# Two attentions in one kernel: one distance table for all heads, and another order of the maxima, inverses and last transfers

## The chip, the cores and the metric

The kernel runs on one core of a Trainium2 chip, as one launch. The core has five engines with queues of their own: PE (TensorE), DVE (VectorE), ACT (ScalarE), POOL (GpSimd) and SP (SyncE, which here only issues transfers). The metric is the device time of one execution in microseconds; of several runs the median is taken.

## The reference

Two transformer blocks work on 1024 tokens of width 1024, in float32. The first block (forgetting attention, a convolution, pooling, a feed-forward part) is not touched. The second has two attentions side by side, whose results go through a gate each, are added and projected:

```
# differential attention, 4 heads, two maps (c) a head, all 1024 keys
s = einsum(q, k) * scale - slope[h] * |qpos - kpos|      # slope[h] = 4 ** -(h + 1)
p = softmax(s);  a = p[0] - lam * p[1];  y_a = rmsnorm(a @ v)
# neighbourhood attention, 8 heads, a grid of 16 x 64 tokens,
# each query sees 8 rows x 16 columns of keys
s = einsum(q, k) * scale + bias[h];  p = softmax(s);  y_b = p @ v
merged = g_a * (y_a @ w_branch_a) + g_b * (y_b @ w_branch_b)
```

## The kernel before, in words

Every engine's program is written out by hand as a sequence of methods, one for each stage (`pe_att2`, `act_att2`, ... and then `pe_na`, `act_na`, ...); semaphores are the only coupling between the engines. An instruction that waits holds everything behind it in its engine's queue. Weights are split into a high and a low part, so that a product of float32 accuracy is three matmuls: `w_load` on SP fetches a tile, `w_high` on ACT rounds it, `w_low` on DVE or POOL takes the rest (`low_engines` says which).

**Differential attention** (`*_att2`). There are 32 units, 8 blocks of 128 queries for each of 4 heads. For each unit PE forms the scores of both maps (16 matmuls), DVE adds the distance table `tab` and takes the row maximum in one instruction (`maxes`, calling `negmax`), ACT takes the exponentials, DVE joins the maps, PE transposes, ACT and DVE copy, PE multiplies with the values. The gate products (`gate_steps`, 24 matmuls a unit, one PSUM bank) lie between these as filling. `tab` holds slope times distance, so each head has another one: SP loads it in `sp_att2` when the last maximum of the head before has read the old one. The queries were scaled in `dve_proj2`.

**Neighbourhood attention** (`*_na`). There are 64 `unit`s (8 blocks of queries for each of 8 heads) that only yield the row maxima: PE forms scores, DVE adds the table `tabS` and takes the maximum. For every four units (a group g) DVE splits the four maxima (`halves`), PE transposes them (`rows` on PE), and DVE writes them (`rows` on DVE) as further rows of the tile `stk`, from which the second pass subtracts them inside the product. The second pass has 96 `step`s, six a group, 12 a head: PE forms transposed scores in one of three banks, DVE adds the table `tabT` (`add`), ACT takes the exponential, and PE multiplies with the values three steps later (`value`), into bank 4 or 5 by group; ACT copies a finished bank (`taken`). Units of group g + 2 are done among the steps of group g, at steps 2 to 5 of the six. From unit 4 on they share banks 6 and 7 with the transposed maxima, and so a unit waits until DVE has read these.

The softmax is divided late: POOL stores a head's row sums to HBM and reads them back spread over the partitions (`sums`), DVE takes the reciprocal (`inverse`), POOL stores it and reads it back broadcast (`inverses`), DVE multiplies (`share`), and every second head ACT and DVE split the result (`high`, `mixed`). All are put at fixed steps.

Between the steps go `branch` parts, by `branch_places`: the norm of the first attention's result and then the 64 parts of its product (`wa`, 16 halves `a` of 4 parts). DVE multiplies each half in bank 3 by its gate half in `gab`, POOL stores it (`scr_yaw`), and only then SP loads the gate half for half a + 2 (`g_load`, `scr_g`). The last 11 parts lie behind the 96 steps, in `branch(192)`. Behind that stands `pe_wb`, the second attention's product and the sum of both; its first parts don't need the last head, its later ones do.

## Time and profile before

| | us |
|---|---|
| median of 3 runs | 3134.53 (3132.15 to 3135.2) |
| the profiled execution | 3132.92 |
| its span | 3131.1 |
| granted clock, mean over the span | 0.965 of full |
| differential attention | about 1586 to 1919 |
| neighbourhood attention | about 1914 to 2175 |
| product of the second branch | about 2175 to 2224 |

A time in the trace counts from the start of the span, on the profiled execution. "Busy" is the time in which an engine's instructions run; for PE it is too high where a matmul stands alone, since the ends are modelled. A wait such as `A <- B` says that A stood until B was done.

### The profile page before, as it was taken

How to read it: one execution, taken by the hardware profiler on the slowest of the kernel's cores; microseconds unless marked ns; L12 is line 12 of the kernel's file. 1: busy time of each engine (PE TensorE's matmuls, PEld its weight loads, DVE VectorE, ACT ScalarE, POOL GpSimd, SP SyncE). 2: the span in 40 equal slices, each digit the busy share in tenths (PEclk: the TensorE clock that was granted, in tenths of full speed). 3: DMA queues.
4: the chain of work that ended last, by engine and by line, in shares of the span. 5: the costliest groups of instructions: out<-in, count | busy, mean ns of one | idle time of the engine just before them, and what ended most of it. 6: DMA issues, size and time to landing. Idle time of an engine off the chain costs nothing.

```text
span 3131.1 us, 31288 instructions
## 1 busy us (share of the span) xinstructions
PE 2934.1 (94%) x13012; PEld 2365.2 (76%) x13012; DVE 1437.4 (46%) x1672; ACT 945.5 (30%) x1193; POOL 360.9 (12%) x309
## 2 busy tenths in 40 slices
PE   7988999999999999899999998887978999999996
PEld 5777767788888888688877786655766888888874
DVE  5775454453535454533244445664554313333335
ACT  3212442221212122311355565432342221111123
POOL 2223111000000000200012221112320000000003
PEclk9999999999999999899999999998998999999997
DMA  2123432111111111246313334553521111111113
GB/s 103 62 74 117 133 92 95 49 46 55 42 53 41 57 38 51 98 141 214 115 64 107 105 104 144 171 163 126 193 88 54 39 56 43 59 34 61 48 60 122
DMA packets 89085, 275.04 MB, mean 88 GB/s; under 512 B 12648, under 2 KB 15336, under 8 KB 88944
## 3 DMA queue, kind: packets, MB, share of 16 engines
q1 hardware_dynamic: 74448, 226.66, 22.2%
q0 software_dynamic: 14496, 46.38, 4.2%
q8 instruction: 103, 1.69, 0.2%
q14 instruction: 38, 0.31, 0.0%
HBM read 220.40 MB, written 52.59 MB: 87 GB/s over the span
## 4 chain that ended last, share of the span: by engine, by line
PE 76%; DVE 8%; ACT 4%; issue 4%; DMA 3%; POOL 1%; SPq 0%; DVEq 0%; ACTq 0%; POOLq 0%
PE ps L206 75%; DVE cacc L177 2%; DVE YA L174 1%; ACT PB L171 1%; PE ps L209 1%; DMA tab<-in_alibi 1%; ACT AH L171 1%; DMA small<-scr_sum 1%; ACT wh L171 1%; DMA scr_sum<-YS 1%; DVE PB L177 1%; DVE stk L174 0%; DVE wl L174 0%; POOL wl L174 0%; DVE XR L174 0%
## 5 line engine op out<-in xcount | busy, mean ns | idle before, releaser
L206 PE MATMUL ps<-AH,wh 128*128 128x512 f32 (+1 forms) x2240 | 900.9, 402 | 80.2 <-DVE wl L174 31.6
L206 PE MATMUL ps<-AL,wh 128*128 128x512 f32 (+1 forms) x2240 | 883.3, 394 | 0.0
L206 PE MATMUL ps<-AH,wl 128*128 128x512 f32 (+1 forms) x2240 | 882.0, 394 | 0.0
L174 DVE TENSOR_TENSOR wl<-raw,wh 128x1024 fp32r<-128x1024 f32 (+2 forms) x240 | 280.5, 1169 | 835.8 <-ACT wh L171 835.6
L206 PEld LDWEIGHTS ps<-AH,wh 128*128 128x128 f32 (+1 forms) x2240 | 425.4, 190 | 190.5 <-issue 41.5
L171 ACT ACTIVATE wh<-raw 128x1024 fp32r<-128x1024 f32 (+2 forms) x289 | 261.8, 906 | 793.6 <-PE ps L206 783.3
L206 PEld LDWEIGHTS ps<-AH,wl 128*128 128x128 f32 (+1 forms) x2240 | 425.6, 190 | 93.3
L206 PEld LDWEIGHTS ps<-AL,wh 128*128 128x128 f32 (+1 forms) x2240 | 426.5, 190 | 90.6 <-issue 3.7
L206 PE MATMUL ps<-UH,wh 128*128 128x512 f32 x880 | 346.8, 394 | 12.6 <-DVE wl L174 7.6
L206 PE MATMUL ps<-UL,wh 128*128 128x512 f32 x880 | 345.1, 392 | 0.0
L206 PE MATMUL ps<-UH,wl 128*128 128x512 f32 x880 | 344.7, 392 | 0.0
L206 PE MATMUL ps<-stk,stk 128*128 128x512 f32 (+3 forms) x832 | 257.6, 422 | 38.8 <-DVE small L186 21.0
L206 PEld LDWEIGHTS ps<-stk,stk 128*128 128x128 f32 x832 | 151.5, 197 | 111.9 <-issue 36.8
L206 PEld LDWEIGHTS ps<-UH,wh 128*128 128x128 f32 x880 | 167.0, 190 | 51.7 <-issue 11.1
L174 POOL TENSOR_TENSOR sqacc<-sqacc,sq 128x512 f32<-128x512 f32 (+1 forms) x51 | 88.1, 1728 | 934.7 <-ACT sq L171 929.9
L206 PEld LDWEIGHTS ps<-UH,wl 128*128 128x128 f32 x880 | 166.9, 190 | 35.1
L206 PEld LDWEIGHTS ps<-UL,wh 128*128 128x128 f32 x880 | 167.0, 190 | 34.4
L174 POOL TENSOR_TENSOR wl<-raw,wh 128x1024 fp32r<-128x1024 f32 (+3 forms) x49 | 109.0, 2226 | 318.2 <-ACT wh L171 318.1
L177 DVE SCALAR_TENSOR_TENSOR cv<-ub,vec,cv 128x1024 f32<-128x1024 f32 x88 | 113.1, 1285 | 55.2 <-ACT cv L171 53.7
L197 DVE RECIPROCAL small<-small 128x1 f32<-128x1 f32 (+3 forms) x61 | 11.4, 186 | 207.8 <-ACT PB L171 129.8
L177 DVE SCALAR_TENSOR_TENSOR cacc<-hp,vec,cacc 128x1024 f32<-128x1024 f32 x60 | 102.0, 1700 | 1.8
L213 POOL DMA_DIRECT2D scr_x<-XR x8 | 4.5, 565 | 715.1 <-DVE XR L174 715.1
(198 smaller groups left out, 3113.4 us busy)
## 6 DMA issues: line engine op xcount, KB each, us to landing
raw<-in_w_up SPq DMA_DIRECT2D x44, 512.0 KB, 3.3
raw<-in_w_gu SPq DMA_DIRECT2D x44, 512.0 KB, 3.2
raw<-in_w_w2in SPq DMA_DIRECT2D x32, 512.0 KB, 4.2
raw<-in_w_down SPq DMA_DIRECT2D x56, 256.0 KB, 2.6
raw<-in_w_down SPq DMA_DIRECT2D x32, 320.0 KB, 2.8
xin<-in_xT SPq DMA_DIRECT2D x16, 512.0 KB, 4.4
stk<-scr_ka SPq DMA_DIRECT2D x32, 256.0 KB, 8.0
raw<-in_w_w2v SPq DMA_DIRECT2D x16, 512.0 KB, 3.3
```

Of the source, the lines that this page charges most:

```text
L171: return Issued(self, self.e.activation(out, in_, func, **kw))
L174: return Issued(self, self.e.tensor_tensor(out, a, b, op))
L177: return Issued(self, self.e.scalar_tensor_tensor(out=out, in0=a, scalar=s, in1=b, op0=op0, op1=op1))
L197: return Issued(self, self.e.reciprocal(out, a))
L206: return Issued(self, self.e.matmul(out, l, r, start=start, stop=stop))
L209: return Issued(self, self.e.transpose(out, a, ident))
L213: return Issued(self, self.e.dma_start(out, in_))
```

## The change

One table of distances (4^-1 times distance) serves all four heads: the queries of head h are scaled by a further 4^h, and the maximum is taken with a scale of -4^-h, so that the sum comes out as before. The gate's fifth step (k = 4) of the last unit moves from the next stage to behind its transposes. In the neighbourhood attention `na_behind` gives the places of units, halves, transposes and rows; the transposed maxima go to banks 4 and 5. Inverses, shares and second splits come some steps later. Behind the steps POOL does the last head's sums and inverse ahead of its branch parts, DVE has an order written out by hand, half 14 of the branch product gets bank 2, and one low part moves from POOL to DVE. The loads of the next stage wait for the last broadcast.

```diff
@@ -116,7 +116,7 @@
     for s in range(len(TILES)):
-        on = "p" if 1 <= s <= TILE["wout", 0] or g0 < s <= wb0 else "d"
+        on = "p" if 1 <= s <= TILE["wout", 0] or g0 < s < wb0 else "d"
         count[on] += 1
@@ -181,9 +181,9 @@
-    def negmax(self, out, a, b, low):
-        return Issued(self, self.e.tensor_tensor_reduce(out=out, in0=a, in1=b, scale=-1.0, scalar=3.0e38, op0=ALU.add,
+    def negmax(self, out, a, b, low, scale=1.0):
+        return Issued(self, self.e.tensor_tensor_reduce(out=out, in0=a, in1=b, scale=-scale, scalar=3.0e38, op0=ALU.add,
                                                         op1=ALU.min, accum_out=low))
@@ -1597,7 +1597,8 @@
             q.wait_ge(S.bl, n - 1)
-            q.stt(self.T2[b][:, :], self.pair(b), 0.125 if key[0][0] == "q" else 1.0, self.RB[:, :], ALU.mult,
+            scale = {"qa": 0.125 * 4.0 ** key[1], "qb": 0.125}
+            q.stt(self.T2[b][:, :], self.pair(b), scale[key[0]] if key[0] in scale else 1.0, self.RB[:, :], ALU.mult,
                   ALU.mult).then_inc(S.bev)
@@ -1637,9 +1638,10 @@
                 self.stack_load(q, self.stk2[2], 2, "qa", "ka", S.dstk2)
-                q.dma(self.tab[:, :], self.io["alibi"][0, :, :]).then_inc(S.dtab0, 16)
+                q.dma(self.tab[:, :], self.io["alibi"]).then_inc(S.dtab0, 16)
         for key in self.SWEEPS2:
@@ -1700,8 +1702,7 @@
             turn(u)
-            if u < 31:
-                self.gate_steps(q, u, 4, 8)
+            self.gate_steps(q, u, 4, 8 if u < 31 else 5)
         value(15)
@@ -1762,13 +1763,14 @@
                 q.wait_ge(S.sc, 64 + 2 * u + c + 1)
-                q.wait_ge(S.dtab0, 16 * (h + 1))
+                q.wait_ge(S.dtab0, 16)
                 q.wait_ge(S.dqs0, 256)
...
                 q.wait_ge(S.cc, u - 1)
-                q.negmax(self.PB2[j][:, :], self.pair(c), self.tab[:, at:at + NTOK], m[:, 0:1]).then_inc(S.mx)
+                q.negmax(self.PB2[j][:, :], self.pair(c), self.tab[:, at:at + NTOK], m[:, 0:1],
+                         4.0 ** -h).then_inc(S.mx)
@@ -1842,9 +1844,6 @@
                 self.w_load(q, TILE["w2in", ("g", u // 2)] + 3)
-            if i == 7 and h < 3:
-                q.wait_ge(S.mx, 64 + 2 * (u + 1) + 2)
-                q.dma(self.tab[:, :], self.io["alibi"][h + 1, :, :]).then_inc(S.dtab0, 16)
         self.na_tab(q, 0)
@@ -1927,7 +1926,7 @@
         S = self.S
-        q.wait_ge((S.dtab0, S.dtab1)[h % 2], (64 if h % 2 == 0 else 0) + 32 * (h // 2) + 16 * part)
+        q.wait_ge((S.dtab0, S.dtab1)[h % 2], (16 if h % 2 == 0 else 0) + 32 * (h // 2) + 16 * part)
@@ -1952,9 +1951,23 @@
+    @staticmethod
+    def na_behind(n):
+        g, r = n // 6, n % 6
+        unit = n + 4 if n < 12 else 4 * g + 8 + r if r < 4 and g < 14 else None
+        halved = {4: 1, 8: 2, 12: 3}[n] if n in (4, 8, 12) else g + 2 if r == 4 and 2 <= g < 14 else None
+        turned = {4: 1, 9: 2, 12: 3}[n] if n in (4, 9, 12) else g + 2 if r == 5 and 2 <= g < 14 else None
+        rows = {5: 1, 10: 2, 13: 3}[n] if n in (5, 10, 13) else g + 1 if r == 1 and 3 <= g < 15 else None
+        return unit, halved, turned, rows
...
-        return self.bank((4, 5)[g] if g < 2 else 6)
+        return self.bank((4, 5, 4, 4)[g] if g < 4 else 4 + (g + 1) % 2)
+    def wa_out(self, a):
+        return self.bank(2 if a == 14 else 3)
@@ -1969,7 +1982,6 @@
                 q.wait_ge(S.ya, 16)
-                q.wait_ge(S.qmr, 8 + u // 4 if u >= 12 else 0)
             out = self.na_out(u)
@@ -1982,6 +1994,8 @@
             self.turned_wait(q, self.CN2 + 63)
+            q.wait_ge(S.qmr, 8 + g)
+            q.wait_ge(S.tyc, 8 + (g - 2 if g >= 4 else 1 if g > 1 else 0))
             q.transpose(self.na_turned(g)[:, 0:128], f32(self.mcN[:, :]), self.ident).then_inc(S.mtr)
@@ -2004,7 +2018,7 @@
             q.wait_ge(S.vone, 2)
-            q.wait_ge(S.qmr, 8 + 2)
+            q.wait_ge(S.qmr, 8 + (g + 1 if g < 2 else min(g + 2, 16)))
             q.wait_ge(S.tyc, 8 + g - 1)
@@ -2033,35 +2047,35 @@
                     q.wait_ge(S.bspl, k + 1)
-                    q.wait_ge(S.wsm, a)
-                    ws = slice(k * P, k * P + P)
-                    q.mm(self.bank(3), h[:, ws], self.Ah[k][:, HALF[half]], k == 0, False)
-                    q.mm(self.bank(3), h[:, ws], self.Al[k][:, HALF[half]], False, False)
-                    i = q.mm(self.bank(3), l[:, ws], self.Ah[k][:, HALF[half]], False, k == 3)
+                    q.wait_ge(S.wsm, a - (a == 14))
+                    if a == 14:
+                        q.wait_ge(S.tad, 96)
+                    ws, out = slice(k * P, k * P + P), self.wa_out(a)
+                    q.mm(out, h[:, ws], self.Ah[k][:, HALF[half]], k == 0, False)
+                    q.mm(out, h[:, ws], self.Al[k][:, HALF[half]], False, False)
+                    i = q.mm(out, l[:, ws], self.Ah[k][:, HALF[half]], False, k == 3)
                     if k == 3:
...
             unit(u)
-            self.gate_steps(q, 31, 4 + u, 5 + u)
-        unit(4)
+            if u < 3:
+                self.gate_steps(q, 31, 5 + u, 6 + u)
         rows(0)
-        for u in (5, 6, 7):
-            unit(u)
         for n in range(99):
-            g = n // 6
+            u, _, g, _ = self.na_behind(n)
             if n < 96:
                 step(n)
-                if n % 6 > 1 and g < 14:
-                    unit(4 * g + 6 + n % 6)
+                if u is not None:
+                    unit(u)
                 branch(2 * n)
...
                 branch(2 * n + 1)
-            if n % 6 == 0 and g < 15:
-                rows(g + 1)
+                if g is not None:
+                    rows(g)
         branch(192)
@@ -2113,8 +2127,8 @@
                 branch(2 * n + 1)
-            if n >= 37 and n % 24 == 13:
-                high((n - 37) // 24)
+            if n >= 43 and n % 24 == 19:
+                high((n - 43) // 24)
         branch(192)
@@ -2181,6 +2195,12 @@
+        def product(a):
+            n, half = a // 2, a % 2
+            q.wait_ge(S.gem, GEM[TILE["wa", n], half])
+            q.wait_ge((S.dsp0, S.dsp1)[half], 48 + 16 * (n + 1))
+            q.tt(self.gab[half], self.wa_out(a), self.gab[half], ALU.mult).then_inc(S.wsm)
@@ -2203,41 +2223,37 @@
                 if part == "wa" and b == 3:
-                    n, half = a // 2, a % 2
-                    q.wait_ge(S.gem, GEM[TILE["wa", n], half])
-                    q.wait_ge((S.dsp0, S.dsp1)[half], 48 + 16 * (n + 1))
-                    q.tt(self.gab[half], self.bank(3), self.gab[half], ALU.mult).then_inc(S.wsm)
+                    product(a)
...
         halves(0)
-        unit(4)
         rows(0)
-        for u in (5, 6, 7):
-            unit(u)
-        halves(1)
         for n in range(96):
-            g = n // 6
+            u, halved, _, g = self.na_behind(n)
             add(n)
-            if n % 6 > 1 and g < 14:
-                unit(4 * g + 6 + n % 6)
-            if n % 6 == 0 and 1 <= g < 15:
-                halves(g + 1)
+            if u is not None:
+                unit(u)
+            if halved is not None:
+                halves(halved)
+            if g is not None:
+                rows(g)
             branch(2 * n)
-            if n % 6 == 1 and g < 15:
-                rows(g + 1)
-            if n >= 18 and n % 12 == 6:
-                inverse((n - 18) // 12)
-            if n >= 24 and n % 12 == 0:
-                share((n - 24) // 12)
-            if n >= 38 and n % 24 == 14:
-                mixed((n - 38) // 24)
+            if n >= 22 and n % 12 == 10:
+                inverse((n - 22) // 12)
+            if n >= 30 and n % 12 == 6:
+                share((n - 30) // 12)
+            if n >= 44 and n % 24 == 20:
+                mixed((n - 44) // 24)
             branch(2 * n + 1)
+        product(13)
+        self.w_low(q, TILE["wb", 0])
         share(6)
-        branch(192)
         inverse(7)
+        product(14)
+        product(15)
         share(7)
@@ -2267,7 +2283,7 @@
                     n, half, k = a // 2, a % 2, b
-                    if half == 0 and k == 2:
+                    if half == 0 and k == 2 and n < 7:
                         self.w_low(q, TILE["wa", n] + 1)
@@ -2277,12 +2293,12 @@
                 sums((n - 15) // 12)
-            if n >= 19 and n % 12 == 7:
-                inverses((n - 19) // 12)
+            if n >= 23 and n % 12 == 11:
+                inverses((n - 23) // 12)
             branch(2 * n + 1)
-        branch(192)
         sums(7)
         inverses(7)
+        branch(192)
@@ -2420,6 +2436,7 @@
             q.wait_ge(S.wsm, 16)
+            q.wait_ge(S.dinv, 32 * 16)
             q.wait_ge(S.dyw0, 16 * (n + 1))
@@ -2579,7 +2596,7 @@
         S = self.S
-        return (S.dstk0, S.dstk1, S.dtab0, S.dtab1)[n % 4], (864, 864, 192, 128)[n % 4]
+        return (S.dstk0, S.dstk1, S.dtab0, S.dtab1)[n % 4], (864, 864, 144, 128)[n % 4]
@@ -3039,11 +3056,8 @@
-    al = np.zeros((4, P, 1920), np.float32)
     dist = np.abs(np.arange(P)[:, None] + 896 - np.arange(1920)[None, :]).astype(np.float32)
-    for h in range(4):
-        al[h] = -(2.0 ** (-8.0 * (h + 1) / 4)) * dist
-    a["alibi"] = al
+    a["alibi"] = -(2.0 ** (-8.0 / 4)) * dist
```

## Rows read from the trace of the kernel before

**Rows 1.** The page, engines: busy us, share of the span, instructions.

```profile
PE 2934.1 (94%) x13012; PEld 2365.2 (76%) x13012; DVE 1437.4 (46%) x1672; ACT 945.5 (30%) x1193; POOL 360.9 (12%) x309
```

**Rows 2.** The chain of waits in the differential attention: start us, us, what.

```profile
1642.28 10.75 PE ps L206 x48
...
1689.41 10.74 PE ps L206 x48
...
1729.81 10.74 PE ps L206 x48
...
1775.90 10.75 PE ps L206 x48
...
1816.30 10.75 PE ps L206 x48
...
1858.41 10.75 PE ps L206 x48
```

**Rows 3.** Waits in the differential attention: us, times, longest.

```profile
DVE PB L186 <- DMA tab<-in_alibi: 16.4, 3, 6.4
```

**Rows 4.** Windows: length, busy PE, PEld, DVE, ACT, POOL, clock, DMA share, GB/s.

```profile
1972.35:1989.47 17.12, 15.33 (x72) 12.07 (x71) 11.48 (x26) 8.93 (x14) 1.08 (x2) 0.80 0.06 17
2028.18:2043.10 14.92, 10.82 (x44) 7.26 (x43) 7.85 (x19) 3.74 (x7) 2.76 (x5) 1.00 0.45 172
2043.10:2054.84 11.74, 11.33 (x47) 7.78 (x46) 8.92 (x19) 4.12 (x8) 2.34 (x3) 1.00 0.96 272
2054.84:2072.04 17.20, 13.60 (x44) 9.26 (x43) 8.23 (x19) 4.26 (x8) 3.42 (x5) 0.80 0.29 108
2084.74:2099.54 14.80, 12.38 (x44) 8.30 (x43) 8.07 (x20) 4.26 (x8) 2.88 (x4) 0.88 0.44 167
2111.98:2123.11 11.13, 10.58 (x44) 7.22 (x43) 8.12 (x21) 4.26 (x8) 3.54 (x6) 1.00 0.31 96
```

**Rows 5.** Waits in the neighbourhood attention: us, times, longest.

```profile
DVE small L197 <- DMA small<-scr_sum: 24.6, 6, 12.1
...
PE ps L206 <- DVE stk L174: 14.5, 10, 3.4
```

**Rows 6.** Timeline of the tail: start, us, what, [idle before <- releaser].

```profile
2142.43 0.60 ACT L171 ACTIVATE YS<-ps 128x512 f32<-128x512 f32 x1 [2.27 <-PE ps L206]
...
2145.51 0.54 POOL L213 DMA_DIRECT2D scr_yaw<-yb  x1 [4.65 <-DVE yb L174]
...
2153.72 0.51 POOL L213 DMA_DIRECT2D scr_sum<-YS  x1
2159.86 0.58 POOL L213 DMA_DIRECT2D small<-scr_sum  x1 [5.63 <-DMA scr_sum<-YS]
...
2167.43 0.53 POOL L213 DMA_DIRECT2D RBc<-scr_inv  x1 [1.41 <-DMA scr_inv<-small]
...
2164.98 0.20 DVE L197 RECIPROCAL small<-small 128x8 f32<-128x8 f32 x1 [12.10 <-DMA small<-scr_sum]
2170.74 1.22 DVE L174 TENSOR_TENSOR RBc<-YS,RBc 64x1024 f32<-64x1024 f32 x1 [5.56 <-DMA RBc<-scr_inv]
...
2175.06 0.77 PE L206 MATMUL ps<-AH,wh 128*128 128x512 f32 x1 [18.82 <-DVE wl L174]
```

**Rows 7.** Timeline of the prologue, SyncE and VectorE.

```profile
1928.85 0.37 SPq L213 DMA_DIRECT2D tabT<-in_nak  x1
...
1935.48 0.69 DVE L174 TENSOR_TENSOR XT<-ps,tabT 128x512 f32<-128x512 f32 x1
```

**Rows 8.** The tile tabT, before 1934 us.

```profile
DMA to landing us min/median/max: 4.3/4.3/4.3
```

**Rows 9.** The tile tabS, whole span: ns min/median/max.

```profile
L186 DVE CUSTOM_DVE_ANT_0 ps<-ps,tabS x64: 685/761/833, 1923.8 to 2121.1; 128x512 f32<-128x512 f32 x32, 128x640 f32<-128x640 f32 x32
...
DMA to landing us min/median/max: 5.2/9.0/13.7
```

**Rows 10.** Timeline of SyncE in the loop.

```profile
2083.46 0.38 SPq L213 DMA_DIRECT2D tabS<-in_na  x1
```

## The prediction

> **What bounds the kernel now.** The page first: PE is busy 94% of the span [rows 1], so time is to be had only where PE stands still, or runs at its lower clock, and the change touches one stretch of that kind, from the differential attention at 1586 us to the restart of the branch products at 2175 us. Three views show three kinds of loss in it.
>
> In the differential attention the chain of waits has a beat: the group of 48 matmuls begins every 20.20 us, two units of work (1689.41 to 1729.81 is 40.40, two beats) [rows 2]. Three beats are longer, and the waits say why: VectorE stood 16.4 us in 3 stalls for the distance table [rows 3].
>
> In the neighbourhood loop no engine is full. Groups of six steps take 11.1 to 17.2 us [rows 4]. The undisturbed ones, such as 2043.10 to 2054.84, take 11.7 with VectorE 8.9 and PE 11.3 busy (PE's busy time is inflated where matmuls stand alone, its weight loads are busy 7.8). The long ones have VectorE standing in the reciprocal for a transfer (24.6 us in 6 waits, the longest, 12.1, in the tail: 12.5 in the loop) and PE standing for the rows that VectorE writes into `stk` (14.5 us in 10 waits) [rows 5], and two of them have a granted clock of 0.80, a part of them at 1.2 GHz after PE stood still [rows 4].
>
> In the tail PE stands 18.8 us in one piece, to 2175.06 [rows 6]. Behind that is a chain: POOL issues head 7's row sums at 2153.72 although ScalarE had copied them by 2143.03, because the stores of the branch products stand ahead of them in POOL's queue; readback at 2159.86, reciprocal at 2164.98, broadcast issued at 2167.43, share at 2170.74, then the two splits and the weight's low half [rows 6].
>
> **Part 1, one table.** Three of four table loads go, and the maximum is scaled by 4^-h instead, in the same instruction, and the queries by 4^h, also in an instruction that is there: 0 us added, 64 maxima and 16 scalings unchanged in number and shape. Removed: from 1642.28 to 1689.41, from 1729.81 to 1775.90 and from 1816.30 to 1858.41 the chain needed 47.13, 46.09 and 42.11 for two beats that elsewhere take 40.40 [rows 2]: 6.73 + 5.69 + 1.71 = 14.1 us. That is less than the 16.4 that VectorE stood, since PE had gate matmuls to do under the start of each stall, and it includes what the clock lost afterwards. What is late next is the ordinary beat itself. The stack loads for the head after next stay where they are, with a whole head (four beats, 81 us) to land in. I take -14, bounds -14.5 and -11 (if a stack or weight load were hidden under the stall).
>
> **Part 2, the seam.** One of four gate steps (3 matmuls at 0.23 us, 0.7 us) moves from behind the last value product to ahead of it, where PE waits about a microsecond for the copies: -0.7. The neighbourhood prologue keeps units 0 to 3 and the first rows; units 4 to 7 go into steps 0 to 3. The first addition ran at 1935.48; its key table was issued at 1928.85 [rows 7] and landed in 4.3, at 1933.2 [rows 8]. That issue stands behind the last store of the differential attention, which a slightly earlier gate moves forward by about 1 us, so the first addition can come at about 1932, 3.5 us sooner. But 12 units instead of 8 now lie in the first two groups, and a unit's maximum is 0.76 us of VectorE [rows 9] and the read of its result 0.14: 3.6 us given back where VectorE has no room, nothing where it has (it waited for PE between the small steps). Of 4.2 gained I keep 2. Bounds -5 and +2, the latter if `rows` for group 1, which now has its transpose in step 4 and its product in step 5 right ahead of step 6, stalls each engine once more.
>
> **Part 3, the loop.** Reciprocals come 4 steps later (n = 22 + 12h instead of 18), shares 6, the second split 6. The sums are issued at step 15 + 12h; from there to the reciprocal were 3 steps, some 6 us, for a round trip of about 10 (in the tail 2153.72 to 2164.96 [rows 6]); now it is 7 steps, some 14 us. So the stalls go whole. The shares then have 7 steps for the inverse's store and broadcast (from the reciprocal at 2164.98 to the share at 2170.74, 5.8 us [rows 6]), and the copies of the next head but one stand two steps behind the share that frees their buffer: no new wait. POOL's `inverses` moves with them, and what queues behind it there is a branch store or a weight's low half, each with a tile's time (about 19 us) to spare. Compare groups: the odd ones take 14.92, 17.20, 14.80 and 11.13, the last with 0.6 of stall, thus 10.5 undisturbed; together 58.05 - 42.0 = 16 over that level. The group at 1972.35 took 17.1 with 11.5 of VectorE work at clock 0.80 [rows 4]; at 14.0 it gives 3. Together 19. The new places of the maxima (units in steps 0 to 3, where value products are small, instead of 2 to 5; the turned maxima in a value bank, so that no unit waits for `rows`) take a PE wait of a few tenths to a microsecond from each of 12 groups: 0.5 each, 6 us. What they add is waits on the copy of a value bank three steps earlier, met by then. I take -25. Bounds: -12, if only the 12.5 of reciprocal stalls goes and all else stays; -38, if eleven groups came down to the 10.3 of the densest work.
>
> A rule speaks here against me. In the loop the granted clock was 1.00 in undisturbed groups in spite of PE pauses up to 1 us at every step, and below it only in groups with a long stall [rows 4]. The Trainium skill, "TensorE: Matmul & The Clock Gate", section "A second HAM failure mode: psum-queue depth-cycling", says that frequent small idle times between groups of matmuls, with the banks cycled, make the clock swing between its two levels by themselves; the steps here cycle three banks. By the trace the clock's loss goes with the stalls; by the rule it stays, and that is the first rival.
>
> **Part 4, the tail.** Now POOL does sums and inverse of head 7 first, and the branch stores last. Sums at 2143.1 instead of 2153.7; with the old durations (to the readback 6.1, to the reciprocal 5.1, to the broadcast 2.5, landing 3.3) readback 2149, reciprocal 2153.5 to 2154, broadcast 2156, landed 2159.5. VectorE meanwhile does product 13, then stands in `inverse(7)` with products 14 and 15 behind it. PE has product 14 ready in its own bank by 2147.2, and then waits for the evacuation: about 7 us idle; product 15 (12 matmuls, 2.7 us, up to 5.5 at 1.2 GHz) ends at 2157 to 2160. A second wait is new: the gate half for product 15 is loaded only when the store of product 13 has landed, and that store is now behind the broadcast in POOL's queue: issued 2156.5, landed 2158.8, load landed about 2162 (before, the store went at 2145.51 [rows 6]). So product 15 ends at about 2162.7, share at 2164, both splits and the low half as before 4.3 us later: PE restarts at about 2167 instead of 2175. The 18 matmuls that are possible before fit in 2160 to 2165, so what follows restarts at the full clock more likely than now, worth up to 2. The low half that moves to VectorE is 0.7 us in its waiting time. The first loads of the mixing stage wait for the last broadcast and product 15 and go at 2163 instead of 2153, used from 2171: 8 us for what landed within 4 to 9. I take -10; bounds -13 (the gate half is no wait) and 0 (these loads are late).
>
> **Sum.** 14 + 3 + 25 + 10 = 52 against the profiled execution's own 3132.9, thus 3081. The median of the runs is 1.6 higher, 3134.5, so I forecast 3082.5 for a median. Everything behind 2190 us is untouched.
>
> **Rivals,** each with the time of a median.
> First, the loop gives little: the clock goes on falling by itself (the rule above), or the reciprocal wait is replaced by one on a bank or table. For it: VectorE waits for PE in nearly every step. Against: the undisturbed groups are already the pattern that is left. Loop -12, the rest as above: 39 less, 3095.
> Second, the tail only shifts: the new order puts VectorE's wait ahead of two products and the gate half behind a store, so that PE's idle time is split and the clock is low for more of it. For it: the wait for the store above. Tail 0: 42 less, 3092.
> Third, slower: the loads of a head's table become the bound of the loop. `tabS` is issued by SP behind the gate halves, in the trace as late as 2083.46 for step 62 [rows 10], and landing takes 5.2 to 13.7 us [rows 9]; the first unit of the head needs it two steps earlier than before, and the steps are faster. At the old pace it had 17 us; now about 13. A stall begins where issue is 4 us later or landing exceeds 13, and it comes out slower than before only if each of six heads stands 9 us or more. Price at 10 us a head: 60 against 52 gained, 3143. Against: the transfers' share in an undisturbed group is only 0.31 to 0.96 [rows 4], and a single late landing costs 1 to 3.
> Fourth, the table's stall was not the table's (a queue behind it holds all): 14 come back, 3096. Against: [rows 3] name the transfer, all three times at a head's start.
>
> **Chances.** Forecast (3070 to 3091) 0.60; first rival 0.15; second 0.08; third 0.03; fourth 0.03; more than forecast, down to 3060, 0.06; both of the first two 0.05 (3105). Range 3063 to 3106. What a measurement of this kernel tells from no change is about 0.2%, 6 us. Faster 0.95, same 0.02, slower 0.03.
>
> **What would show it.** No wait on `tab`, and a beat of 20.20 through all heads. Reciprocals in the loop without a transfer as releaser; groups of 10 to 12.5 us; clock near 1.00 from 1950 on. In the tail sums right behind the copy, PE idle twice (about 7, then a few us) instead of 18.8 once. Wrong would be: an XT or `ps` wait on `tabS` or `tabT`, groups still over 14 us, or PE restarting later than 10 us behind the broadcast's landing.

## The result, and the profile after

The changed kernel takes 3095.65 us (median of 4 runs, 3094.52 to 3098.76), the kernel before, on the same chip, 3134.86. The ratio is 0.9878, with a 95% interval of 0.9861 to 0.9895: 39.2 us less, where 52 had been forecast. The profiled execution took 3094.52 (span 3092.7, mean granted clock 0.969), and the lines of this section are its trace against the one of before. One execution of e11, an experiment further down, ran in a slow state (4194.22 us at a mean granted clock of 0.65) and is left out of its median; all others compared here are fast.

The page's engines, which answer to [rows 1]:

```profile
PE 2924.6 (95%) x13012; PEld 2357.9 (76%) x13012; DVE 1434.8 (46%) x1673; ACT 944.8 (31%) x1193; POOL 360.3 (12%) x308
```

The work is the same; what has changed is where it stands still. Four checkpoints divide the gain. The first maximum of the differential attention comes at 1584.05 (before 1586.09; nothing ahead of it was changed, so its 2.0 us are scatter). From there to the first addition of group 2 of the neighbourhood loop it is 358.10 us (before 372.69), from there to the loop's last addition 170.94 (before 180.75), from there to the product of the second branch 30.29 (before 42.31). That is 14.6 + 9.8 + 12.0 = 36.4 us, and with the scatter the 38.4 by which the spans differ. Behind that checkpoint both take the same (949.3).

The chain of waits in the differential attention, which answers to [rows 2], now has the one beat of 20.20 us throughout, and the wait of [rows 3] is gone:

```profile
1640.26 10.74 PE ps L206 x48
1660.46 10.75 PE ps L206 x48
1680.66 10.74 PE ps L206 x48
1700.86 10.75 PE ps L206 x48
1721.06 10.74 PE ps L206 x48
```

The seam, SyncE and VectorE (start, us, what, and in brackets the idle time and what ended it), to compare with [rows 7]. The first addition is 3.3 us earlier, counted from the first maximum and without the table's part, and now waits for its table, which lands 4.4 us behind its issue (4.3 before, [rows 8]):

```profile
1911.63 0.37 SPq L213 DMA_DIRECT2D tabT<-in_nak  x1
...
1912.87 0.69 DVE L174 TENSOR_TENSOR stk<-ps,cst 64x512 fp32r<-64x512 f32 x1 [0.42 <-PE ps L209]
1916.06 0.69 DVE L174 TENSOR_TENSOR XT<-ps,tabT 128x512 f32<-128x512 f32 x1 [2.50 <-DMA tabT<-in_nak]
```

Windows of five groups of the loop (columns as in [rows 4]), groups 3 and 8 to 11. The long ones of 14.92, 17.20 and 14.80 that a transfer had stopped (groups 7, 9 and 11 of before) are 11.95, 11.67 and 14.27 now; but no group with maxima in it is shorter than 11.6 us, group 3 is still 17.2 at a clock of 0.80, and the ones that had been undisturbed have not gained (group 8, 11.74 before, is 12.03):

```profile
1956.08:1973.26 17.18, 15.44 (x72) 11.89 (x71) 11.12 (x26) 9.16 (x14) 0.99 (x2) 0.80 0.01 0
...
2022.29:2034.32 12.03, 11.07 (x47) 7.86 (x46) 7.71 (x18) 4.15 (x8) 2.88 (x4) 1.00 0.88 217
2034.32:2045.99 11.67, 10.94 (x44) 7.14 (x43) 8.75 (x20) 4.15 (x8) 1.66 (x3) 1.00 0.55 210
2045.99:2058.61 12.62, 11.06 (x47) 7.86 (x46) 7.75 (x18) 3.63 (x7) 2.91 (x4) 1.00 0.71 194
2058.61:2072.88 14.27, 12.54 (x44) 8.17 (x43) 10.13 (x22) 5.17 (x9) 2.86 (x4) 0.88 0.46 166
```

The waits of the neighbourhood attention in the kernel after (us, times, longest), to compare with [rows 5]: of 24.6 us for the row sums 1.2 are left (in the tail), and PE's 14.5 us for `stk` don't appear. In their place stands a wait for L186, the maximum of a unit (PEld, the weight loads, and PE, the matmuls, overlap, so the two rows are not added up):

```profile
PEld ps L206 <- DVE small L186: 28.0, 28, 2.9
...
PE ps L206 <- DVE small L186: 16.5, 23, 2.4
...
DVE small L197 <- DMA small<-scr_sum: 1.2, 1, 1.2
```

The same view of before has less than half of it:

```profile
PEld ps L206 <- DVE small L186: 11.8, 13, 1.6
...
PE ps L206 <- DVE small L186: 6.7, 11, 1.3
```

The tail after, to compare with [rows 6]. POOL issues the sums at 2118.18; readback, reciprocal, inverse and broadcast follow within 8 us. VectorE then stands 8.4 us before the last product, until its gate half has landed, and PE, which had stood 18.82 us once, stands 3.53 and 3.52:

```profile
2118.18 0.50 POOL L213 DMA_DIRECT2D scr_sum<-YS  x1
...
2121.44 0.59 POOL L213 DMA_DIRECT2D small<-scr_sum  x1 [2.77 <-DMA scr_sum<-YS]
2123.40 0.20 DVE L197 RECIPROCAL small<-small 128x8 f32<-128x8 f32 x1 [1.17 <-DMA small<-scr_sum]
...
2124.22 0.80 PE L206 MATMUL ps<-AH,wh 128*128 128x512 f32 x1 [3.53 <-DVE yb L174]
...
2125.87 0.54 POOL L213 DMA_DIRECT2D RBc<-scr_inv  x1 [1.42 <-DMA scr_inv<-small]
2126.40 1.11 POOL L213 DMA_DIRECT2D scr_yaw<-yb  x2
...
2132.59 0.69 DVE L174 TENSOR_TENSOR yb<-ps,yb 128x512 f32<-128x512 f32 x1 [8.41 <-DMA yb<-scr_g]
...
2137.63 0.77 PE L206 MATMUL ps<-AH,wh 128*128 128x512 f32 x1 [3.52 <-DVE wl L174]
```

### The profile page after: what moved, and what is told of

It reads as the page before. It is cut to its first block, busy times and chain, and to the rows that moved or that the text cites. A ratio compares the mean times of both kernels' runs of the same rounds, so it can differ in the third digit from the quotient of the medians.

```text
span 3092.7 us, 31280 instructions
## 1 busy us (share of the span) xinstructions
PE 2924.6 (95%) x13012; PEld 2357.9 (76%) x13012; DVE 1434.8 (46%) x1673; ACT 944.8 (31%) x1193; POOL 360.3 (12%) x308
## 4 chain that ended last, share of the span: by engine, by line
PE 78%; DVE 9%; ACT 4%; issue 3%; DMA 1%; POOL 1%; SPq 0%; DVEq 0%; POOLq 0%; ACTq 0%
PE ps L206 77%; DVE cacc L177 1%; DVE YA L174 1%; ACT PB L171 1%; PE ps L209 1%; ACT AH L171 1%; DVE PB L177 1%; DVE ps L186 1%; DVE stk L174 1%; DVE XT L174 1%; DVE wl L174 0%; ACT wh L171 0%; DVE XR L174 0%; DMA raw<-in_w_w2out 0%; DVE AL L177 0%
## 5 line engine op out<-in xcount | busy, mean ns | idle before, releaser
L206 PE MATMUL ps<-stk,stk 128*128 128x512 f32 (+3 forms) x832 | 250.9, 413 | 24.7 <-DVE small L186 21.7
L197 DVE RECIPROCAL small<-small 128x1 f32<-128x1 f32 (+3 forms) x61 | 11.3, 186 | 193.3 <-ACT PB L171 139.5
```

Source lines behind the costliest of these rows:

```text
L197: return Issued(self, self.e.reciprocal(out, a))
L206: return Issued(self, self.e.matmul(out, l, r, start=start, stop=stop))
```

## The experiments

Twelve runs (e1 to e12) were made in three sessions, each beside the kernel before on the same chip; the changed kernel's own result has a session of its own, in which the kernel before took 3134.86. Ratios are to the kernel before of the session; "loop" is the time from the first to the last addition of the 96 steps in the profiled execution, "tail" from there to VectorE's first product of the second branch. Loop and tail are read from one trace a kernel. Four traces with the changed kernel's loop (changed, e4, e5, e8) have 197.0 to 197.6, so there the loop is read closely. Two with the loop of before (before, e1) have 204.05 and 209.2: where transfers stop it, it is not. Medians are compared within a session, ratios across; where e3 and e4 are set against the changed kernel both are given.

| kernel | median us | ratio (95%) | loop | tail |
|---|---|---|---|---|
| before | 3134.3, 3136.5, 3133.6 | 1 | 204.05 | 42.3 |
| changed | 3095.65 | 0.9878 (0.9861 to 0.9895) | 197.03 | 30.3 |
| e1 one table alone | 3119.55 | 0.9953 (0.9936 to 0.9970) | 209.2 | 41.2 |
| e2 old order of maxima | 3091.72 | 0.9864 (0.9844 to 0.9885) | 191.2 | 30.2 |
| e3 early inverses | 3096.77 | 0.9886 (0.9868 to 0.9904) | 206.9 | 29.0 |
| e4 old tail | 3108.27 | 0.9925 (0.9904 to 0.9946) | 197.5 | 46.3 |
| e5 changed again | 3095.53 | 0.9867 (0.9850 to 0.9883) | 197.06 | 32.2 |
| e6 maxima spread | 3077.94 | 0.9814 (0.9797 to 0.9831) | 179.9 | 30.0 |
| e7 maxima late | 3086.27 | 0.9846 (0.9827 to 0.9865) | 189.6 | 30.2 |
| e8 another tail | 3092.88 | 0.9863 (0.9848 to 0.9878) | 197.6 | 25.7 |
| e9 spread and tail | 3077.58 | 0.9825 (0.9800 to 0.9849) | 179.1 | 29.5 |
| e10 narrow units in one bank | 3089.21 | 0.9862 (0.9841 to 0.9884) | 193.8 | 31.9 |
| e11 all three | 3073.89 | 0.9810 (0.9787 to 0.9834) | 178.4 | 27.5 |
| e12 splits late, units not | 3093.94 | 0.9878 (0.9855 to 0.9901) | 196.0 | 32.3 |

### The parts, one by one (first session)

**e1** is the kernel before with one table (the edits to `alibi`, `negmax`, the queries' scale and the counts of its semaphore, nothing else).

> The kernel before with the one distance table alone. My theory, from the chain of waits in both traces (14.1 us between the same two places): 3134.9 - 14 = 3120.7, 3119 to 3122.5. Rival (the table's stall hid other loads that now come late, or the saving is partly the clock's and comes back elsewhere): 3124 or more.

Measured: 14.7 us less than before, inside the 3119 to 3122.5 that had been expected. Its waits have none for `tab`. The theory of the table holds, and the fourth rival falls.

**e2** is the changed kernel with the places of units, halves and rows of before (prologue too) and the turned maxima in bank 6; late inverses and the new tail stay.

```diff
-        return self.bank((4, 5, 4, 4)[g] if g < 4 else 4 + (g + 1) % 2)
+        return self.bank((4, 5)[g] if g < 2 else 6)
...
-                if u is not None:
-                    unit(u)
+                if n % 6 > 1 and g < 14:
+                    unit(4 * g + 6 + n % 6)
```

> The changed kernel with the old places of the maxima, halves and rows (units in steps 2 to 5, turned maxima in bank 6, units 4 to 7 and the gate's fifth step in the prologue). Theory A: the new order gained nothing in the loop, because four units in four steps running through one pair of banks make PE wait for each maximum, and VectorE then stands at the end of the group: 3095.6, within 3 either way; groups of six steps 11.5 to 12.5 us, waits PE <- small shorter and PE <- stk longer than in the changed kernel. Rival B (my prediction's term): the new order is worth 6 us and more, 3101 to 3104.

Measured: no loss at all; by the ratios it is 4.4 us below the changed kernel, with intervals that overlap, so rival B falls. Its loop is 5.8 us shorter than the changed kernel's (4.6 of them from group 2 on), though it has PE's waits for `stk` (4.6 us), which the new order takes away; its wait for the maxima is 6.4 us against 16.5. The first addition comes 4.7 us later (336.7 against 332.0 behind the first maximum), since four more units stand ahead of it. So the new order of the loop takes away a wait and brings a larger one, and from the first maximum to the last addition the two orders differ by 1.2 us only.

**e3** puts inverses, shares and second splits back to their early steps.

```diff
-            if n >= 22 and n % 12 == 10:
-                inverse((n - 22) // 12)
+            if n >= 18 and n % 12 == 6:
+                inverse((n - 18) // 12)
```

> The changed kernel with reciprocals at step 18 + 12h, shares at 24, splits at 37 and 38 as before. Theory A (the late inverses are the whole of the loop's gain of about 10, the stalls of 12.5 us come back): 3106 to 3110, VectorE again waiting for small<-scr_sum 10 to 13 us in the loop and one or two more stretches at 1.2 GHz. Rival B (the order carries part of the gain, the stalls hide behind PE): 3098 to 3102.

Measured: 3096.77, below what both theories gave (3106 to 3110, 3098 to 3102), and by the ratios 2.5 us above the changed kernel, within the intervals. In its profiled execution (the slowest of its five, 3102.08) the loop is 9.9 us longer, and the transfer stops VectorE again, 9.5 us in 4 places. These are the two longest; the group around the second takes 16.06 us:

```profile
2013.14 0.20 DVE L197 RECIPROCAL small<-small 128x8 f32<-128x8 f32 x1 [3.11 <-DMA small<-scr_sum]
...
2041.99 0.20 DVE L197 RECIPROCAL small<-small 128x8 f32<-128x8 f32 x1 [4.41 <-DMA small<-scr_sum]
```

So with the new order the late inverse is worth between 3 and 10 us; the two figures were not reconciled. With the old order it is worth more: from e1 to e2 the medians fall by 27.8 us, and less the tail's share (11.0 by the two traces, 14.7 by the ratio of e4) 13 to 17 remain; the loop falls from 204.05 or 209.2 to 191.2.

**e4** puts the tail back (bank, order on DVE and POOL, the low part).

> The changed kernel with the old tail: POOL's branch stores ahead of head 7's sums, product 14 in bank 3, the first low half of the next stage on POOL, no wait of the mixing loads. By the distance from the last addition to PE's restart (35.5 us before, 24.5 after) the tail is worth 11: 3106 to 3108, PE idle 18 to 19 us in one piece. Rival: the late mixing loads and the split idle time give part of it back later, 3100 to 3103.

Measured: by the medians 12.6 us above the changed kernel (by the ratios 14.7), where the forecast had given the tail 10. PE stands again in one piece:

```profile
2119.65 1.22 DVE L174 TENSOR_TENSOR RBc<-YS,RBc 64x1024 f32<-64x1024 f32 x1 [7.65 <-DMA RBc<-scr_inv]
...
2152.04 0.76 PE L206 MATMUL ps<-AH,wh 128*128 128x512 f32 x1 [18.02 <-DVE wl L174]
```

Not all of it is the old tail's. e4 keeps the late inverses, so VectorE stands 7.65 us for head 6's broadcast before it comes to the products behind the steps (the first line; in the kernel before it stood 0.25), and e4's tail of 46.3 us is 4.0 longer than the 42.3 of before.

### Why the loop gave little (second and third session)

What the first session left open was why groups of 12 us stay where no transfer and no row stops them. One group of the changed kernel in VectorE's timeline, 2045.99 to 2058.61:

```profile
2046.60 0.69 DVE L186 CUSTOM_DVE_ANT_0 ps<-ps,tabS 128x512 f32<-128x512 f32 x1
...
2048.62 0.69 DVE L186 CUSTOM_DVE_ANT_0 ps<-ps,tabS 128x512 f32<-128x512 f32 x1
...
2051.33 0.82 DVE L186 CUSTOM_DVE_ANT_0 ps<-ps,tabS 128x640 f32<-128x640 f32 x1
...
2052.86 0.83 DVE L186 CUSTOM_DVE_ANT_0 ps<-ps,tabS 128x640 f32<-128x640 f32 x1 [0.24 <-PE ps L206]
...
2054.70 0.42 DVE L174 TENSOR_TENSOR XT<-ps,tabT 128x256 f32<-128x256 f32 x1 [0.95 <-PE ps L206]
...
2056.43 0.29 DVE L174 TENSOR_TENSOR XT<-ps,tabT 128x128 f32<-128x128 f32 x1 [1.02 <-PE ps L206]
2058.61 0.69 DVE L174 TENSOR_TENSOR XT<-ps,tabT 128x512 f32<-128x512 f32 x1 [1.89 <-PE ps L206]
```

PE in the same group:

```profile
2052.27 0.56 PE L206 MATMUL ps<-stk,stk 128*128 128x512 f32 x2 [1.56 <-DVE small L186]
```

Four maxima stand in four steps in a row. In step 3 PE waits 1.56 us, until VectorE has done the maximum of step 2, which stands in its queue behind the write of `stk`, a branch product and an addition; then come two steps with little for VectorE and much for PE, and VectorE stands 0.95, 1.02 and 1.89 us. Neither engine is full, each waits for the other in its turn.

**e5** is the changed kernel again, as the session's own measure. **e6** spreads the maxima and lets splits and transposes follow:

```diff
-        unit = n + 4 if n < 12 else 4 * g + 8 + r if r < 4 and g < 14 else None
-        halved = {4: 1, 8: 2, 12: 3}[n] if n in (4, 8, 12) else g + 2 if r == 4 and 2 <= g < 14 else None
-        turned = {4: 1, 9: 2, 12: 3}[n] if n in (4, 9, 12) else g + 2 if r == 5 and 2 <= g < 14 else None
+        unit = n + 4 if n < 12 else 4 * g + 8 + (0, 2, 4, 5).index(r) if r in (0, 2, 4, 5) and g < 14 else None
+        halved = {4: 1, 8: 2, 12: 3}[n] if n in (4, 8, 12) else g + 2 if r == 5 and 2 <= g < 14 else None
+        turned = {4: 1, 9: 2, 12: 3}[n] if n in (4, 9, 12) else g + 1 if r == 0 and 3 <= g < 15 else None
```

**e7** has the same with the units in steps 2 to 5 (`4 * g + 6 + r if r > 1`).

> The changed kernel once more, unedited, beside the three below, since the kernel before alone spread over 16 us on the last chip. 3092 to 3097; groups of six steps 11.7 to 12.7 us, two of them about 17 and 14.

> The changed kernel with the four maxima of a group at steps 0, 2, 4 and 5 instead of 0 to 3 (halves at 5, transpose at 0, rows at 1). Theory A: in the changed kernel one pair of banks serves four maxima in four consecutive steps, PE stands 1.5 to 1.9 us for a maximum at step 3 and VectorE 3.8 us at steps 4, 5 and 0; spread over the light steps too, groups take 11.0 instead of 12.1 and the kernel is 8 to 12 us faster than e5, 3083 to 3088. Rival C: a group is bound by the round trip of its six steps through three banks, wherever the maxima stand; within 3 us of e5.

> The changed kernel with its new prologue and value banks for the turned maxima, but the maxima at steps 2 to 5 as before from group 2 on. Theory A: the prologue is worth 4 to 5 us (first addition 330.7 us after the start of the differential attention, 335.4 with the old one) and the old places in the loop 4 to 6, both now together: 5 us faster than e5, 3088 to 3091. Rival: places don't matter, and what made e2 faster was bank 6 or chance; within 2 us of e5.

Measured: e6 is 17.6 us faster than e5, e7 9.3, more than the 8 to 12 and the 5 that had been expected. By where they stand, the same maxima are worth as much as the late inverses are with the old order. e7 shows that it is not closeness alone: it too has four maxima in four steps in a row, but in those in which VectorE's additions are small, and its loop is 7.5 us shorter than e5's; spreading them gives 9.6 more. VectorE's timeline of the group of e6 that does the same work (2031.51 to 2042.42, 10.91 us for 12.62) shows no idle piece over 0.85 us:

```profile
2032.12 0.69 DVE L186 CUSTOM_DVE_ANT_0 ps<-ps,tabS 128x512 f32<-128x512 f32 x1
...
2036.30 0.69 DVE L186 CUSTOM_DVE_ANT_0 ps<-ps,tabS 128x512 f32<-128x512 f32 x1
...
2037.94 0.42 DVE L174 TENSOR_TENSOR XT<-ps,tabT 128x256 f32<-128x256 f32 x1 [0.48 <-PE ps L206]
2038.28 0.82 DVE L186 CUSTOM_DVE_ANT_0 ps<-ps,tabS 128x640 f32<-128x640 f32 x1
...
2040.01 0.29 DVE L174 TENSOR_TENSOR XT<-ps,tabT 128x128 f32<-128x128 f32 x1 [0.85 <-PE ps L206]
2040.35 0.83 DVE L186 CUSTOM_DVE_ANT_0 ps<-ps,tabS 128x640 f32<-128x640 f32 x1
...
2042.42 0.69 DVE L174 TENSOR_TENSOR XT<-ps,tabT 128x512 f32<-128x512 f32 x1 [0.77 <-PE ps L206]
```

Its windows have the same work in 11 to 12 us, and the group that was at 0.88 of the clock (14.27) is at 1.00 (12.08):

```profile
2031.51:2042.42 10.91, 10.91 (x47) 7.86 (x46) 7.85 (x19) 3.59 (x7) 2.89 (x4) 1.00 0.76 202
2042.42:2054.50 12.08, 10.42 (x44) 7.41 (x43) 10.40 (x21) 5.21 (x9) 2.91 (x4) 1.00 0.66 216
```

e6 differs from e5 in two things, and could work in two ways. **e12** keeps the units in steps 0 to 3 and only moves splits and transposes as in e6. **e10** keeps the changed order and takes away a part of the wait on the banks: units that are 512 wide take bank 6 or 7 in turn instead of the pair.

```diff
+        if u >= 4 and u % 8 in (0, 1, 6, 7):
+            return self.bank(6 + u % 2)[:, 0:self.na_geo(u % 8)[1] * 128]
...
-            q.wait_ge(S.mx, 128 if u < 2 else 128 + u - 1 if u < 4 else 128 + u)
+            q.wait_ge(S.mx, 128 if u < 2 else 128 + u - 1 if u < 4 or u > 6 and u % 8 in (0, 1, 7) else 128 + u)
```

> Control for e6: units stay in steps 0 to 3, only the splits of the maxima go from step 4 to 5 and their transposes from step 5 to step 0 of the next group, as they stand in e6. Theory (the spread of the units makes e6's gain): at most 3 us off the changed kernel, 3092 to 3096, the group lengths stay near 12. Rival (the later splits and transposes make it, since the transpose waited for them in step 5): near e6, 3078 to 3083, groups near 11.

> The changed kernel's order, only the narrow units (512 wide, 4 of 8 a head) take one bank of the pair, 6 or 7 in turn; three units of a head then need not wait for the maximum of the unit before. If the wait of TensorE for the maximum is what costs (theory: one pair of banks for units in consecutive steps), its waits, 16.5 us in 23 places over the stage, fall by about a third to a half, and the loop gives 4 to 8 us: 3088 to 3092. Rival: the loss is VectorE's own queue, in which an addition stands behind a maximum whose scores come late; then the waits only change their name and the time stays at 3095.

Measured: e12 is the changed kernel (ratio 0.9878, loop 196.0, the waits for maxima 15.8 us in 22 places): the splits are not it, the places of the units are. e10 takes 3.3 us from the loop, where 4 to 8 had been expected; its time is 4.7 below e12's, with intervals that overlap. PE's waits for maxima fall from 16.5 in 23 places to 13.9 in 17, and what is left are the waits of the five units of a head that still need the maximum of the unit before:

```profile
PE ps L206 <- DVE small L186: 13.9, 17, 2.3
```

The first group gained 1.4 us, and groups 9 and 13, in which a pause of PE of 0.3 us went, 0.5 and 0.6 (11.67 to 11.17, 11.64 to 11.04); group 10, shown above, gained nothing: the 1.56 us before the wide unit stay, and its length is 12.62 in both. So the banks of the narrow units have a small share. The wide units could not be given other banks, since there are only these two, so the share of their wait by itself was not measured. Shown is that other places for the maxima, with the same banks, take 17.1 us from the loop; that what is late behind the close maxima is VectorE's own queue is read from the timeline above and was not tried by itself.

### The tail once more, and all together

**e8** lets POOL store product 13 between the two transfers of the sums, and puts product 14 ahead of the reciprocal on VectorE; **e9** is e6 with that, **e11** e9 with the banks of e10.

```diff
+            if h == 7:
+                store(13)
             q.wait_ge(S.dsum, 32 * (8 + h) + 16)
```

> The changed kernel with two moves in the tail: POOL stores product 13 between the two transfers of head 7's sums, and VectorE does product 14 ahead of the last reciprocal. By the trace, the gate half of product 15 was waited for 8.4 us, because it follows that store. It should land by the time PE has finished product 15, share 7 comes 4 us earlier: 3.5 to 4.5 us faster than e5. Rival: the mixing loads, which wait for product 15 and the last broadcast, or the clock after PE's idle time take it back; within 1.5 of e5.

> The changed kernel with the maxima spread over steps 0, 2, 4 and 5 (as in e6) and the tail of e8 together. If the two gains are independent, the sum of 17.6 and 2.7 us comes off the changed kernel's 3095.5: about 3075 (3070 to 3080), a ratio to the kernel before of 0.9806, the restart of the second branch's product about 4 us earlier behind the last step than in the changed kernel. Rival: the tail's 2.7 us was the scatter between executions, then the ratio stays at e6's 0.9814.

> e9 and e10 together. With the maxima already spread, a unit finds its banks free in nearly all steps (1.1 us of such waits in e6), so the single banks add nothing: within 3 us of e9, about 3075. By the rival that VectorE's queue is the limit it is the same; a further gain of 5 us or more would say that spreading had not removed the wait.

Measured: in e8 the wait for the gate half is gone, and the last product waits for PE alone:

```profile
2127.29 0.69 DVE L174 TENSOR_TENSOR yb<-ps,yb 128x512 f32<-128x512 f32 x1 [2.94 <-PE ps L206]
2129.85 1.22 DVE L174 TENSOR_TENSOR RBc<-YS,RBc 64x1024 f32<-64x1024 f32 x1 [1.87 <-DMA RBc<-scr_inv]
```

The tail is 4.6 us shorter than in the changed kernel's trace and 6.5 shorter than in e5's (which are the same kernel); the median is 2.7 below e5's, inside the intervals, where 3.5 to 4.5 had been expected. In e9 little of it is left: the broadcast of head 7 landed late (VectorE waited 2.90 us for it, at 2115.90, where e8 waited 1.87), the tail is 29.5, and the ratio is no better than e6's. So the rival expectation, that 2.7 us was scatter, can't be turned away. e11 has the shortest loop (178.4) and a tail of 27.5. At 3073.89 it is the fastest kernel here, 1.9% below the one before and by the ratios (0.9810 to 0.9878) 21 us below the changed one. It is 3.7 us below e9, where at most 3 had been expected, 0.7 of it in the loop and 2.0 in the tail; against e6 and e9 the intervals don't tell it apart.

## Why the prediction was right, and where it was not

The measured 3095.65 lies above the forecast's own band (3070 to 3091, chance 0.60) and where the first rival stood (3095, chance 0.15). In Parts 1, 2 and 4 cause and direction were right; Part 3 has one term too large and one with the wrong sign, and the sum was 12.8 us too large, nearly all of it by these two. Of the signs that the text itself had named for being wrong two are there: groups over 14 us (17.18 and 14.27), and an `XT` wait on `tabT`, 2.50 us before the first addition. The clock, too, was not near 1.00 throughout.

**Part 1, right to the tenth.** The beats gave 14.1 where 14 was taken from [rows 2]; no beat, load or stack came late behind the stall. e1, alone, 14.7.

**Part 2, the gain was there and was spent.** The first addition came 3.3 us earlier (the forecast said 3.5), held by the landing of its table as written. But the 12 units in the first two groups cost what the text had set against it: these groups take 26.1 us instead of 23.3. At the start of group 2 0.5 us are left. The text kept 2 of 4.2, in which the gate step's 0.7 is already contained, and then put 3 into its sum; by its own working the sum was 51.

**Part 3, the term that was mis-sized.** From group 2 on the loop gave 9.8, with the first two groups 7.0, where 25 had been taken. e2, which has the late inverses but the old order, divides it in two. From group 2 to the last addition the kernel before took 180.75, e2 166.38 and the changed kernel 170.94 (one trace each; e1, with the same loop as before, 185.91).

The first two terms were to give 19, and gave 14.4 (19.5 if e1 is the measure). The transfer's stalls, 12.5 us, went whole, as forecast. What did not come is the rest: the level of 10.5 us to which four groups were to sink was read from one group, 11.13 minus its stall. In e2, where nothing stalls them, the same four (7, 9, 11 and 13) take 11.83, 11.23, 12.11 and 11.23, 4.4 us over 42.0, and group 3, from which 3 us were to come, takes 17.13. Taking the shortest group for the level of all was the smaller error.

The larger one is the half microsecond a group for the new places of the maxima, which has the wrong sign: 4.6 us lost from group 2 on instead of 6 gained. The text priced the wait that this order removes (for `stk`; 4.6 us are left of it in e2) and called what it adds "met by then", looking at the value banks. It did not ask what the unit behind the unit waits for: the same pair of banks, until VectorE, busier in those steps, has taken the maximum. e6 shows how much lay there: with the same maxima at other steps the loop is 17.1 us shorter.

**The first rival had the mechanism in part,** and the time by luck. It said 3095 for a loop that gives 12 because a wait is replaced by one on a bank, or because the clock falls by itself. The time was 3095.65, and the wait for the maxima is such a one; but the loop gave 9.8 and the seam 0.5 instead of 3, and the tail 2.0 more and the scatter of the first 1586 us another 2.0 made it up.

As to the clock: in the loop of the kernel after it falls twice to 1.2 GHz, for 6.8 us in group 3, at the end of a pause of PE of 1.40 us (to 1963.33), and for 3.4 us in group 11, behind pauses of 0.56 and 1.04 us (to 2064.47). No transfer holds VectorE there. Yet behind pauses of 1.41 us (group 2) and 1.56 us (group 10) it stays at 1.00, and so it does in group 11 of e6 behind a pause of 1.66 us (to 2047.48).

The section "A second HAM failure mode: psum-queue depth-cycling" of the Trainium skill's "TensorE: Matmul & The Clock Gate", which lets the clock swing by such small pauses, is thus borne out in groups 3 and 11, and not in groups 2 and 10. The prediction, which gave the loss of clock to long stalls alone, was wrong by the trace it had: in the kernel before the clock also fell in group 3 behind a pause of 1.79 us and in group 4 behind one of 1.30, both waits for `stk` with no transfer in them, and the undisturbed group of 11.74 us has no PE pause over 0.31, not one of up to 1 us at every step. In group 2 or 3 the clock falls in every kernel here, for 3.4 us in e6 and e9 and for 6.8 in most others. In most it falls within 2 us of a pause of 1.2 to 1.8 us, in e9 it does so (at 1964.5) with no pause over 0.3 us in the 13 us before; what makes it fall there was not found.

**Part 4, right.** PE restarts 24.5 us behind the last addition instead of 35.5: 11 for 10 (in e5, the same kernel, its second pause is 5.46 us and the tail 1.9 longer). The new wait for the gate half is there (8.4 us on VectorE) with the cause that was named, POOL's store behind the broadcast; PE's idle time is 3.5 and 3.5 instead of 7 and some, since the round trip of the sums was quicker (2118.18 to 2123.40, 5.2 us where 11 had been taken from [rows 6]). The 1.0 more that the next stage gained goes with its clock: behind the restart PE is at 1.2 GHz for some 3 us instead of 5; the restart at the full clock, which the text had thought more likely than before, did not come. The late loads of the mixing stage cost nothing that shows. The second and third rival fall: the tail gave 12, and nothing waits for `tabS`.

In sum 14.1 + 0.5 + 9.8 + 12.0 + 2.0 of scatter, against 14 + 3 + 25 + 10.

## What to carry to other kernels

Two engines that hand work to each other in order through two or three banks, as here, do not run at the pace of their average work: before work is put together in a few steps, add up what each engine has in each step, put the additional work where the engine has little (e7), and spread it so that neither is the late one twice running (e6). When a wait is removed, ask for the instruction that uses the same buffer next, and who has to be done by then. And a group's "undisturbed" length is to be read from its median or its own idle times, never from the shortest one.

## What was not expected of the hardware

The stretch ahead of the first change, 1586 us with the same instructions in all kernels, ended between 1575.4 (e2) and 1586.1 us (before), while the changed kernel's loop repeats within 0.6 us in four traces (197.03 to 197.64), and the loop of before, which transfers stop, within 5 only. A single trace's total is thus good to some 5 us and a stage of it to far less, and small gains are to be read by stage. The round trip of head 7's sums, two transfers of 4 KB, took 11.3 us before (2153.72 to 2164.98 [rows 6]) and 5.2 after, from the same instructions; its first half, on which POOL waits, 5.63 and 2.77. In e1 and e4, which have the old order of the tail, that wait is 5.10 and 5.09. What differs is what stands ahead: in these three a product's store of 256 KB is issued 0.5 us before it (in e4 2130.97 and 2131.50), in the kernel after the last one 5.0 us before. In e8, where such a store is issued 0.8 us behind the sums, the readback follows them in 3.3 us as in the kernel after. That the store ahead is the cause was not tried by itself. A small transfer's duration is thus not to be carried from one order to another.
